# Shift and scale in column halves, half of the first attention projection between them, and two of sixteen partial sums on TensorE

## What is computed

```python
mod = silu(c) @ w_ada + b_ada                    # c: 1 x 2048, w_ada: 2048 x 12288
shift1, scale1, gate1, shift2, scale2, gate2 = split(mod, 6)
h = rms_norm(x, norm1_w) * (1 + scale1) + shift1 # 256 x 2048
proj = h @ w_in                                  # w_in: 2048 x 7168
aq, ak, av, gq, gf, gi, gg = split(proj)         # attention q, k, v and four parts of a gated recurrence
aq, ak = rope(rms_norm(aq)), rope(rms_norm(ak))  # per head of 128
...
x = x + gate1 * (concat(attn, hg) @ w_out)
```

## Time and profile before

| | |
|---|---|
| median of 3 runs | 2480.05 us (2479.54 to 2480.23) |
| the profiled execution | 2479.47 us, span 2477.7 us |
| TensorE busy | 2330.2 us (94%), 10802 instructions |
| VectorE busy | 1603.8 us (65%) |
| ScalarE busy | 1037.0 us (42%) |
| TensorE waits over 3 us after 123 us | before x is turned in `mlp` 6.4; gates 5.9; `mix_part(3)` 5.7; A_lo 5.2 in three; first recurrent level at 489.5, 4.0; softmax 3.9 in five |

### The profile page before, as it was taken

How to read it: one execution, slowest core, us unless ns; L and a number is a source line. 1 busy time by engine, 2 the same in 40 slices (tenths; PEclk the granted TensorE clock), 3 DMA queues, 4 the chain that set the end, 5 groups by cost and what they waited for, 6 DMA issues and landing times.

```text
span 2477.7 us, 27782 instructions
## 1 busy us (share of the span) xinstructions
PE 2330.2 (94%) x10802; PEld 1938.8 (78%) x10802; DVE 1603.8 (65%) x1277; ACT 1037.0 (42%) x878; POOL 67.0 (3%) x63
## 2 busy tenths in 40 slices
PE   0399999998999999999998999999999999999999
PEld 0377888786888888888886888878888888888887
DVE  7789989766566666665557555555655555555554
ACT  1164553433433333333333466565443343433432
POOL 0010000000000000000003000000000000000000
PEclk9999999998999999999999999999999999999999
DMA  7798997743566667565553654534555555555552
GB/s 295 329 370 325 333 328 264 248 159 119 197 234 233 235 237 239 202 196 189 190 186 119 204 164 159 168 128 156 182 189 189 193 187 186 188 185 193 195 186 102
DMA packets 230883, 519.15 MB, mean 210 GB/s; under 512 B 9689, under 2 KB 10146, under 8 KB 224162
## 3 DMA queue, kind: packets, MB, share of 16 engines
q1 hardware_dynamic: 230818, 518.27, 61.2%
HBM read 516.14 MB, written 2.10 MB: 209 GB/s over the span
## 4 chain that ended last, share of the span: by engine, by line
PE 83%; DVE 9%; issue 2%; ACT 2%; DMA 2%; DVEq 1%; POOL 1%; ACTq 1%; SPq 0%
PE PS L237 26%; PE PS L239 26%; PE PS L238 26%; DVE ada_acc L989 2%; DVE w_lo L227 2%; DVE MS L949 2%; PE PS L1467 2%; DMA ada_raw<-in_w_ada_dram 1%; PE PS L1506 1%; POOL rstd L524 1%; PE PS L276 1%; ACT w_hi L223 1%; DVE rt L853 0%; ACTq L314 0%; PE PS L1450 0%
## 5 line engine op out<-in xcount | busy, mean ns | idle before, releaser
L227 DVE TENSOR_TENSOR w_lo<-raw,w_hi 128x2048 fp32r<-128x2048 f32 x392 | 897.8, 2292 | 705.6 <-ACT w_hi L223 700.1
L223 ACT ACTIVATE w_hi<-raw 128x2048 fp32r<-128x2048 f32 x392 | 750.9, 1916 | 1128.2 <-PE PS L239 1128.2
L237 PE MATMUL PS<-w_hi,A_hi 128*128 128x512 f32 x2112 | 834.4, 395 | 9.9 <-DVE A_lo L329 5.2
L239 PE MATMUL PS<-w_hi,A_lo 128*128 128x512 f32 x2112 | 824.4, 390 | 0.0
L238 PE MATMUL PS<-w_lo,A_hi 128*128 128x512 f32 x2112 | 824.0, 390 | 0.0
L237 PEld LDWEIGHTS PS<-w_hi,A_hi 128*128 128x128 f32 x2112 | 398.2, 189 | 91.6 <-issue 7.5
L239 PEld LDWEIGHTS PS<-w_hi,A_lo 128*128 128x128 f32 x2112 | 397.6, 188 | 83.9
L238 PEld LDWEIGHTS PS<-w_lo,A_hi 128*128 128x128 f32 x2112 | 398.2, 189 | 80.4 <-issue 0.5
L237 PE MATMUL PS<-w_hi,H_hi 128*128 128x512 f32 x1024 | 402.3, 393 | 0.1
L239 PE MATMUL PS<-w_hi,H_lo 128*128 128x512 f32 x1024 | 399.0, 390 | 0.0
L238 PE MATMUL PS<-w_lo,H_hi 128*128 128x512 f32 x1024 | 398.5, 389 | 0.0
(11 more groups left out here) (260 smaller groups left out, 1140.3 us busy)
## 6 DMA issues: line engine op xcount, KB each, us to landing
raw<-in_w_ff_dram SPq DMA_DIRECT2D x128, 1024.0 KB, 5.1
raw<-in_mlp_w_in_dram SPq DMA_DIRECT2D x64, 1024.0 KB, 5.5
raw<-in_mlp_w_out_dram SPq DMA_DIRECT2D x64, 1024.0 KB, 4.9
raw<-in_w_in_dram SPq DMA_DIRECT2D x56, 1024.0 KB, 7.9
X<-in_w_ada_dram SPq DMA_DIRECT2D x96, 512.0 KB, 5.9
raw<-in_sb_w_qkv_dram SPq DMA_DIRECT2D x48, 1024.0 KB, 5.1
ada_raw<-in_w_ada_dram SPq DMA_DIRECT2D x32, 1024.0 KB, 7.2
raw<-in_w_out_dram SPq DMA_DIRECT2D x16, 1024.0 KB, 5.0
```

The source lines that it names most:

```text
L223: act.activation(w_hi[:, j, :, :], raw[:, j, :, :], ACT.Copy).then_inc(hi_rdy, 1)
L227: dve.tensor_tensor(w_lo[:, j, :, :], raw[:, j, :, :], w_hi[:, j, :, :].bitcast(F32), ALU.subtract).then_inc(lo_rdy, 1)
L237: pe.matmul(bank(pair + t), h, w_hi[:, j, k, :], start=first, stop=False)
L239: mm = pe.matmul(bank(pair + t), l, w_hi[:, j, k, :], start=False, stop=last)
```

## The change

- The pieces of `w_ada` keep 1 MB, but hold 1024 columns of shift and 1024 of scale: sixteen pieces give the first half of the columns of both, sixteen the second half (`for h`, `for k`).
- Of each sixteen VectorE adds fourteen (`ADA_DVE`); TensorE sums pieces 14 and 15 by itself from `ada_raw` with silu(c) as the column (`piece_sums`), in the order piece 14, `MS`, piece 15. Their buffers are free when TensorE has done so (`ada_pe`). VectorE adds the three columns (`half_modulation`), the first half's behind piece 0 of the second half.
- The turn of x has two halves of four steps. x is normalised in place, the first four steps' transposes are made early. The first attention group is projected in the order `AT0_ORDER`: q, k, v over the first half of the contraction (6 chunks, `HEAD`), then q, k, v over the second. TensorE does the first six between `sums(0)` and `sums(1)`. Loads of `w_in` stand among the pieces (`LOADS_AFTER`), the `w_lo` of chunks 0 to 7 among VectorE's adds (`LOW_AFTER`).
- In the first group q is complete after 8 chunks and k after 10; the steps move to the slots in `at_steps`.
- The 96 pieces of the other modulations start at slot 7, 2 a slot. TensorE's wait before level 1 counts one more `mod_rdy`.
- The masks are made before VectorE waits for TensorE's transposes, the bounds and angles (with the rope tables) behind piece 4; the q and k norms are loaded behind piece 3; positions have a semaphore of their own.

```diff
+AT0_ORDER = [(b, k) for h in range(2) for b in range(3) for k in (2 * h, 2 * h + 1)]
+HEAD = CH * 3 // 2
+ADA_PE = 2
+ADA_DVE = KT - ADA_PE
+LOADS_AFTER = {(0, 9): 0, (0, 11): 1, (0, 13): 2, (1, 0): 3, (1, 2): 4, (1, 4): 5, (1, 6): 6, (1, 9): 7}
+LOW_AFTER = {(0, 11): 0, (0, 13): 1, (1, 1): 2, (1, 3): 3, (1, 5): 4, (1, 7): 5, (1, 9): 6, (1, 11): 7}
...
-        return 3 * x // 2 if x <= CH * 3 else 3 * CH * 3 // 2 + 2 * (x - CH * 3) - sum(v < x for r in LEVEL_SLOTS for v in r)
+        return max(0, 2 * (x - HEAD - 1)) - sum(v < x for r in LEVEL_SLOTS for v in r)
...
+        def at0_chunk(pe, n):
+
+            b, k = AT0_ORDER[n]
+            if b == 0:
+                pe.wait_ge(a_lo, 2 * (k + 1))
+            chunk(pe, n // CH, n % CH, pairs[b], lambda i, t: A_hi[:, CH * k + i, P * t:P * t + P],
+                  lambda i, t: A_lo[:, CH * k + i, P * t:P * t + P], k == 0, k == CH - 1)
...
-            ada = a["w_ada"].rearrange("a (k p) (s n) -> p (a k) s n", p=P, n=D)
-            with sp.Fori(0, 2) as i:
-                for k in range(KT):
-
-                    sp.wait_ge(ada_used, KT * i + k + 1)
-                    sp.dma_start(ada_raw[:, k % CH, :], ada[:, k, i, :]).then_inc(ada_in[k % CH], 16)
...
-                    sp.wait_ge(a_tr, KT // 2)
+                    sp.wait_ge(y_rdy, 4)
...
+            for h in range(2):
+                for k in range(KT):
+                    r = KT * h + k - CH
+                    if r >= 0 and r % KT < ADA_DVE:
+                        sp.wait_ge(ada_used, ADA_DVE * (r // KT) + r % KT + 1)
+                    elif r >= 0:
+                        sp.wait_ge(ada_pe, ADA_PE * (r // KT) + r % KT - ADA_DVE + 1)
+                    sp.dma_start(ada_raw[:, k % CH, :].rearrange("p (s n) -> p s n", s=2),
+                                 ada[:, k, 0:2, D // 2 * h:D // 2 * (h + 1)]).then_inc(ada_in[k % CH], 16)
+                    if (h, k) == (0, CH - 1):
+                        sp.dma_start(wq_b[:, :], a["q_norm_w"].to_broadcast([P, P])).then_inc(bcast_in, 16)
+                        sp.dma_start(wk_b[:, :], a["k_norm_w"].to_broadcast([P, P])).then_inc(bcast_in, 16)
+                        for i, name in enumerate(("q_norm_w", "k_norm_w")):
+                            sp.dma_start(w_cols[:, i:i + 1], a[name].rearrange("a (p b) -> (a p) b", b=1)).then_inc(bcast_in, 16)
+                    if (h, k) in LOADS_AFTER:
+                        load_at0(LOADS_AFTER[h, k])
+            for n in range(len(LOADS_AFTER), CH * 3):
+                load_at0(n)
+
...
+            for slot in range(CH * 2):
+                for q in ada_pieces(slot):
+                    ada_load(q)
...
-                normalise(act, X, Y0, c)
+                normalise(act, X, X, c)
+            for n in (0, 1):
+                split_hi(act, 0, n)
             act.wait_ge(g_rdy, 1)
-            turn_act(act, 0, g1, mod[:, SHIFT1, :], GN, between={1: lambda: split_hi(act, 0, 0), 4: lambda: split_hi(act, 0, 1)})
-            for j in (2, 3):
-                split_hi(act, 0, j)
+            turn_act(act, 0, g1, mod[:, SHIFT1, :], turned, steps=ALL[:4], banks=FIRST)
+            for n in range(2, CH * 2):
+                split_hi(act, n // CH, n % CH)
+            act.wait_ge(g_rdy, 2)
+            turn_act(act, 0, g1, mod[:, SHIFT1, :], turned, steps=ALL[4:], first=4, banks=SECOND,
+                     between={1: lambda: split_hi(act, 2, 0)})
+            split_hi(act, 2, 1)
...
+            def half_modulation(h):
+
+                kts = slice(KT // 2 * h, KT // 2 * (h + 1))
+                n = KT * (1 + ADA_PE)
+                dve.wait_ge(ada_sum, h + 1)
+                dve.wait_ge(ada_pe, ADA_PE * (h + 1))
+                dve.tensor_reduce(ada_part[:, 0, :], bank(6, n * h, n * h + n).rearrange("p (c m) -> p c m", m=1 + ADA_PE),
+                                  AX_X, ALU.add)
+                d()
+                dve.tensor_tensor(mod[:, SHIFT1:GATE1, kts], ada_part[:, 0, :].rearrange("p (s k) -> p s k", s=2),
+                                  colA[:, 0:2 * KT].rearrange("p (s k) -> p s k", s=2)[:, :, kts], ALU.add).then_inc(mod_rdy, 1)
+                d()
+                r0 = RA["norm1"][0]
+                dve.scalar_tensor_tensor(out=g1[:, kts], in0=mod[:, SCALE1, kts], scalar=1.0,
+                                         in1=colA[:, r0 + kts.start:r0 + kts.stop], op0=ALU.add, op1=ALU.mult).then_inc(g_rdy, 1)
...
+                    if (h, k) == (0, 4):
+                        bounds_and_angles()
+                    if (h, k) == (1, 0):
+                        half_modulation(0)
+                    if (h, k) == (1, 1):
+                        turn_first(ALL[0:2], 0)
+                    if (h, k) == (1, 2):
+                        turn_first(ALL[2:4], 2)
+                    if (h, k) in LOW_AFTER:
+                        n = LOW_AFTER[h, k]
+                        split_lo(dve, n // CH, n % CH)
+                    dve.wait_ge(ada_used, ADA_DVE * h + k + 1)
...
+            def half_sums(h, m, column):
+
+                for c in range(KT):
+                    at = (1 + ADA_PE) * (KT * h + c) + m
+                    lhs, rhs = column(c)
+                    mm = pe.matmul(bank(6, at, at + 1), lhs, rhs, start=True, stop=True)
+                return mm
+
+            def piece_sums(h, m):
+
+                k = ADA_DVE + m
+                pe.wait_ge(ada_in[k % CH], 16 * (h * (KT // CH) + k // CH + 1))
+                half_sums(h, 1 + m, lambda c: (ada_raw[:, k % CH, P * c:P * c + P], sc[:, k:k + 1])).then_inc(ada_pe, 1)
+
+            def sums(h):
+
+                piece_sums(h, 0)
+                pe.wait_ge(ada_used, ADA_DVE * (h + 1))
+                half_sums(h, 0, lambda c: (MS[:, h, P * c:P * c + P], ones[:, 0:1])).then_inc(ada_sum, 1)
+                piece_sums(h, 1)
 
...
-            pe.wait_ge(mod_rdy, 1)
-            turn(0, Y0)
+            turn(0, X, steps=ALL[:4], banks=FIRST)
+            pe.wait_ge(ada_used, 1)
+            sums(0)
+            for n in range(HEAD):
+                at0_chunk(pe, n)
+            pe.wait_ge(y_rdy, 4)
+            turn(0, X, steps=ALL[4:5], first=4, banks=SECOND)
+            sums(1)
+            pe.wait_ge(mod_rdy, 2)
+            turn(0, X, steps=ALL[5:6], first=5, banks=SECOND[1:])
+            for i, b in ((6, 7), (7, 6)):
+                pe.wait_ge(a_hi, i - 1)
+                turn(0, X, steps=ALL[i:i + 1], first=i, banks=(b,))
...
+def at_steps(n):
+
+    if isinstance(n, int) and n == 0:
+        return {"square": (8, 10), "norm": (9, 11), "turn": (10, 11), "copy": (11, 12)}
+    return {"square": (4, 8), "norm": (5, 9), "turn": (9, 11), "copy": (10, 11)}
```

More of the change, by code:

```diff
@@ L159, in build @@
         ada_raw = sb("ada_raw", [P, CH, D], c=start)
+        turned = sb("turned", [P, 2, NC_], c=start)
         start.close()
@@ L634, in at_own @@
             def at_own(n, B0, s, by_row=False):
-                if s in (5, 9) and not by_row:
-                    norm_rows(n, s // 8, (QN, KN)[s // 8])
-                if s == 4:
+                steps = at_steps(n)
+                if s in steps["norm"] and not by_row:
+                    which = steps["norm"].index(s)
+                    norm_rows(n, which, (QN, KN)[which])
+                if s == steps["square"][0]:
                     if by_row:
@@ L654, in at_own @@
                     c.then_inc(pair_read[0], 1)
-                if s == 11:
+                if s == steps["copy"][1]:
                     act.wait_ge(n_tr, 2 * n + 2)
@@ new lines, in _ @@
+            d()
+            ROUND = 12582912.0
+            dve.tensor_scalar(kk, ang, float(1 / (2 * np.pi)), ROUND, ALU.mult, ALU.add)
+            d()
+            dve.tensor_scalar(kk, kk, ROUND, None, ALU.subtract)
+            d()
+            c1 = 6.28125
+            c2 = float(np.float32(np.round((2 * np.pi - c1) * 2 ** 21) / 2 ** 21))
+            for c in (c1, c2, float(2 * np.pi - c1 - c2)):
+                dve.scalar_tensor_tensor(out=ang, in0=kk, scalar=-c, in1=ang, op0=ALU.mult, op1=ALU.add)
+                d()
@@ L942, in _, with turn_first @@
+            def turn_first(steps, first, **more):
+                turn_dve(dve, 0, g1, mod[:, SHIFT1, :], turned, steps=steps, first=first, **more)
             for h in range(2):
-                for k in range(KT):
+                for k in range(ADA_DVE):
                     sl = ada_raw[:, k % CH, :]
@@ L965, in scale @@
                                          op0=ALU.add, op1=ALU.mult).then_inc(g_rdy, 1)
-            dve.wait_ge(ada_sum, 2)
-            modulation(SHIFT1, GATE1)
-            scale(g1, SCALE1, "norm1")
+            half_modulation(1)
             def ada_collect(n, acc):
@@ L1180, in _ @@
             for i, (kind, idx, B0, nb) in enumerate(groups):
-                for s in range(CH * nb):
+                for s in range(0 if i else HEAD, CH * nb):
                     if i:
@@ L1581, in _ @@
                 prev_used = list(used)
```

(14 more changed lines are left out.)

160 lines of the change are left out of this document (73 added, 87 removed).

## The result

| | before | after |
|---|---|---|
| median | 2479.84 us (2479.54 to 2480.23) | 2499.27 us (2496.82 to 2500.81) |
| ratio, 95% interval | | 1.0077 (1.0064 to 1.0090) |
| span of the profiled execution | 2477.7 us | 2498.9 us |
| TensorE busy | 2330.2 us | 2369.3 us |
| seventh chunk done | 164.0 | 171.6 |

A forecast was written before the change was run, and what follows sets the result against it. VectorE and the DMA rings bound the kernel before 123 us, TensorE after. Start +4.7, K +3.0 and output projection +8.3 make +16.0 on 2480.05, so 2496 us; own range 2490 to 2503, wider range 2480 to 2505.

The forecast's parts named there:

- a ring that lags: Other modulations' pieces: 96th added in slot 60, not 56, delaying x and position 8's load at the output projection; +8.3 us.
- the stall at K: First attention group: TensorE waits for rotated K before its transposes; +3.0 us, between 0 and 4.
- Part 1: Start of VectorE: mask work moves into idle time, first piece at 24.8 us, a gain of 5.2 if four pieces have landed.
- Part 2: First half of w_ada: piece 14 lands at 65 us, three TensorE sums take 21 until 86, rings run dry.
- Part 3: Second half: VectorE sets the pace, three sums end at 156, seventh chunk starts at 161.2; shift +4.7 with low clock.
- The clock, weighed: Column sums at the start: whether each costs 7.0 us, as traced, or half by the skill's load time; trace row decides.
- faster rival: Both halves' sums at half price, 3.5 us each, at twice the granted clock: total -5.7, 2474.3 us; chance 0.10.
- milder rival: Second half's sums at the upper clock level, seventh chunk about 9.5 us earlier: 2486.6 us; chance 0.11.
- Part 4: Q and K of the first attention group: TensorE reaches K's transposes before K is rotated; stall +3.0 us, 0 to 4.
- Part 5: Output projection: late ring delays x and position 8's load, so gate copies; stall 6.3 plus about 2 low clock, +8.3 us.
- the start costs nothing: Start of the kernel: the halves cost as much as they hide, other two terms stay; 2491.4 us, no separate chance.
- the output projection absorbs the load: Output projection: x and position 8 land by 530, nothing lost there; 2487.8 us, chance 0.12.

The follow-up runs named there:

- (6): Kernel before with only the pieces of w_ada changed to column halves (4 KB rows), VectorE adding all 32: 2481.49 us, 1.0005.
- (7): Changed kernel with the four q and k norm loads ahead of x again instead of behind the fourth piece: 2499.90 us, 1.0082.
- (8): Changed kernel with unread f32 matmuls (12, then 9) ahead of each series of three column sums: 2492.51 us, 1.0052.
- (10): Changed kernel with TensorE summing pieces 5 and 10 of each half, x loaded later, K's transposes later, Q's copy first: 2469.51 us, 0.9958.
- (4): Changed kernel with K's transposes of the first attention group behind the thirteenth chunk instead of the twelfth: 2499.36 us, 1.0085.
- (5): Changed kernel with K's first transposes behind the thirteenth chunk and ScalarE's copy of transposed Q ahead of its scaling of K: 2499.72 us, 1.0079.
- (3): Kernel before with only the other modulations' 96 pieces started at slot 7, two a slot: 2487.91 us, 1.0034.
- (1): Changed kernel with VectorE adding all sixteen pieces of each half, TensorE making one sum a half: 2484.92 us, 1.0020.
- (2): Changed kernel with SyncE's wait for the 96th piece and x's second load moved from ahead of position 8's load to position 12's: 2490.22 us, 1.0048.
- (9): Changed kernel with all adds on VectorE, x loaded later, K's transposes a chunk later and Q's copy first: 2475.76 us, 0.9982.
- (11): The 2469.51 us kernel (TensorE summing pieces 5 and 10) with ten unread matmuls ahead of the first half's last sum: 2471.29 us, 0.9967.

## Why the prediction was right, and where its terms were off

The time (2496 against 2499.3) and the sign came out, with the mechanism named: 42 us of sums in series and a ring that lags. That the total is so near is in part luck, since the start was put 2.9 too low, and the stall at K was added although it is hardly a cost. By its steps:

- **Part 1**, right: first add forecast at 24.8, 24.65 measured. Its proviso that four pieces must have landed held.
- **Part 2**, mechanism right, one term off. The three sums took what the earlier trace rows said, 20.6 us, and the rings ran dry where they should. But piece 14 landed at 68.6, not 65. "The 4 KB rows of the half pieces cost nothing where VectorE or TensorE is last; in the first half at most 1 us" was the failing step: they cost 2.4 in the kernel before (6), and the place of the small loads behind the fourth piece 1.3 (7). Both losses come from edits that I had written off: the one with a bound from a single window of 2 us, the other without a word on the queue. VectorE's own end, put at 62.4, comes to 63.8 by the terms given; nothing hangs on it, since VectorE then waited for pieces until 68.0.
- **Part 3**, right in its course: stall before `w_lo` 4.3 (forecast 4.7), VectorE through at 141.2 (140), sums from 139.3 to 159.9 (135 to 156), mod 160.3 (157). Most of the 3.6 of part 2 went through. The seventh chunk started at 165.0, not 161.2, so 3.8 late. Its low clock cost 1.2, not 2.0: it took 6.6 us from start to end, where 5.44 is usual. Together the shift was 7.6, not 4.7.
- **The clock, weighed**: the row decided rightly for this change. A granted clock of 0.50 stands in both series, and each sum took 6.96. It was what TensorE did ahead of the sums that made it so, as (8) shows: 3.63 at 1.00. The faster rival's condition (a sum under 3.6) is thereby nearly met in a kernel that warms TensorE, but only for the first sum of a series, and a series has three. (Its own time is off by 1.3: from +4.7, with 2.0 and twice 10.5 off, the shift is -18.3, not -17.) The milder rival, chunks just ahead keeping the level, was wrong here, where a gap of 5.24 us stands before 139.29; in (8), where unread matmuls fill the gap, and in (10), where there is none, the first sum behind it took 3.63. The Trainium skill, "TensorE: Matmul & The Clock Gate", section "LDWEIGHTS (loading the stationary operand)", gives 128 / 1.2 = 107 ns for a load of 128 columns. From the start of a sum to the start of what follows it, the traces have 109 ns an instruction at the upper level (3.49 us for 32, 135.77 to 139.26 in (8)) and 213 at the lower (6.82 us, 68.64 to 75.46): the figure agrees with the upper level alone.
- **Part 4**, size right (2.8 against 3.0), meaning wrong. I counted the stall as a cost. It is one only where nothing behind it has slack; (4) and (5) took it away twice and gained 1 us at most, since the softmax's own chain absorbs it. The sum had need of the term all the same: without the stall, (5) is still 10.4 us behind the kernel before at the second group's K, where the start accounts for 7.6. Waits at the softmax up to there, 5.2 us for 3.0 in the kernel before, are most of the rest; the prediction had none.
- **Part 5**, right: x at 537.6, which in the frame of before (less 10) is 527.6 against my 526; position 8 landed 9.6 behind it (10.5); ScalarE's last gate copies ended at 550.6, that is 540.6 (539.6). The loss from the level on was 10.0 in the profiled execution, for 8.3: a stall of 5.0 (6.3), 2.5 of low clock behind it (2.0), and 2.6 ahead of it that I left out, most of it a wait of 1.6 us at the next level. The size is right because these errors partly cancel. That wait appears with the late ring in (3) too.
- **The milder rivals** (the start costs nothing, the output projection absorbs the load) are refuted, the one by the seventh chunk, 7.6 late, and by (1), the other by (2) and (3).

What stays open: the last 1.2 us of the 21.2, spread over the rest of the program, and by what way the small loads cost their 1.3 us (7). That the late ring is worth 9.1 in the changed kernel and 8.0 alone is within the intervals.

## What to carry to other kernels

Work moved to an idle engine is free only if it is not last: two of sixteen pieces cost 14.4 us where TensorE summed them at the end of each half (1), and gained 6.3 where it summed two in the middle of it ((10) against (9)). A wait that a queue makes for one late load holds every load behind it, so put the wait where the data is needed, not where it may first be issued. And a stall seen in the profile is worth its length only if the next chain has no slack; take it away once before you count it.

## What the runs showed of the hardware

- The clock's level decides a column sum's price, 3.63 against 6.96 us for 32 instructions. Behind one sum at the upper level the next, without a gap, was at the lower: granted 0.94 in the first, 0.50 in the second (8). The same showed in the chunk behind a sum in (10) and (11): 0.72 and 0.50 from 121 to 127.
- In the kernel before the column of the granted clock says 1.00 where the sums ran at the lower price (so from 67 to 75 us; the earlier trace rows); in the changed kernel, with a few early transposes at 26, it says 0.50 for the same price. The length of a known instruction is the surer sign.
- Pieces of 1 MB in rows of 4 KB moved at 385 GB/s between 40 and 50 us and at 420 between 80 and 100, those in rows of 8 KB at 419 and 427 in the same windows (6). Between 50 and 60 it was the other way about, 392 and 382; over the whole half the 4 KB rows cost 2.4 us.
- Four loads of small rows, 129 KB in all, issued behind the fourth piece instead of ahead of x made piece 14 land 1.3 us later, though they had landed before the next piece was issued (7).
